# A hybrid decoder step on one core: loads of three stages moved a stage ahead, and the first projection tile copied out of PSUM before it is scaled

## The chip, the cores and the metric

The kernel runs on one core of one Trainium2 chip, as one program in one launch. The metric is the device time of that program in microseconds. Before the change it is 3295.6 us, the median of three runs (3295.22, 3295.60 and 3301.45).

## The reference, cut to what matters

One inference step of a decoder trunk of two layers, for 1024 prompt tokens and 8 sample tokens (one each, with a past of 8192 positions). Layer 0 runs two mixers side by side on one input projection: S5, a diagonal state-space model with 32 groups of 64 states, and multi-head latent attention (MLA) with 16 heads. Layer 1 is windowed attention. Each layer ends in a gated MLP with a short convolution. All is float32. The change lies in layer 0:

```python
h = rmsnorm(x, norm_mix[layer])
z = h @ e_w_in[li]                      # 512 S5 columns, 384 query, 256 key/value latent, 32 rotary
u, xq, xkv, kr = z[..., :o1], z[..., o1:o2], z[..., o2:o3], z[..., o3:]
y_s5, hr, hi = s5_mixer(u, h0_re, h0_im, lam_re, lam_im, log_dt, b_re, b_im, c_re, c_im, d_skip, w_glu, b_glu)
q_nope, q_rope, ckv, k_rope = mla_project(xq, xkv, kr, pos, q_norm, w_uq, kv_norm)
o = mla_prompt_attn(q_nope, q_rope, ckv, k_rope, w_uk, w_uv)
mix = jnp.concatenate([y_s5, o], axis=-1) @ e_w_out[li]
# at the end of s5_mixer:
y = gelu(y); y = y * sigmoid(y @ w_glu + b_glu)
# mla_project normalises both latents:
q = rmsnorm(xq, q_norm) @ w_uq;  ckv = rmsnorm(xkv, kv_norm)
```

## The kernel before, in words

Tokens lie along the free dimension (NT = 1032 columns: 1024 prompt and 8 sample), features along the 128 partitions. The kernel is written by hand, engine by engine: each stage is one block, and in it each engine has its own list of instructions with waits on semaphores. A block ends when all five engines have come to its end, so a stage opens on all engines at nearly one time. SP issues nearly all the DMAs, in the order in which they are written.

The stages that matter, in their order:

1. **First projection** (lines 273 to 462). Ten tiles of 128 columns of the weight matrix. SP loads a tile's weights into one of two slots of `slab_raw` (`Slabs.load`, L111). GpSimd splits them into a high and a low part (`Slabs.split`, L121 and L123) once the products that used the slot are done. TensorE makes three products for each of 8 slices of k and 3 thirds of the tokens (`Slabs.products`, L137 to L139), into one of two PSUM slots, which it takes when `slabs.free` says that the slot was emptied. VectorE empties a tile and scales it by the norm's factor `rstd` in one instruction (`evacuate`, L399). Tile q is computed as column tile (q + 4) % 10, so the latents come first. The norm's sums of squares are made on TensorE (`norm_sums`, L232) between the products of tile 1; their roots on ScalarE (`norm_roots`, L237, three thirds), their reciprocals on VectorE (L244). VectorE's list is then: `evacuate(0)`, six doublings of S5's table of cosines and sines (`double`, L409 to L414), `evacuate(1)`, a doubling, `evacuate(2)`, and so on. `scale` (L422) norms the latents and counts `lat_done`. SP stores the normed latents and the rotated key at the end (L305, L307).
2. **S5** (lines 473 to 793). SP first loads the four parameters `s5_b`, `s5_c`, `s5_d` and `s5_h0` (L503). TensorE waits for all of them (L515), transposes `s5_b` (L518), multiplies the samples by it (64 small matmuls, L523); VectorE waits for that (L656), then builds the tables of powers up to `ca` (L725), for which `slab_raw` serves as scratch. Four rounds of states follow (TensorE L564 to L588, VectorE L743 to L775), then the samples (L602 to L607), and ScalarE's gelu (L627, L631). SP ends with the stores of the states.
3. **Gate** (lines 796 to 832). SP loads the weights and the bias (L804, L805). TensorE waits for both and makes 4 column tiles of the product (L815), ScalarE their sigmoid (L824), VectorE the product with S5's output (L832).
4. **Heads** (lines 848 to 1116). A loop of four rounds with four heads each. SP loads the mask and the rotary table (L895, L896) and, at each round, the round's weights `wq` and `wkv` (L899, L900), once the nine projections of the round before are done (`proj` starts at 1, L918). TensorE waits for the weights (L935), projects queries (L924), keys (L931) and values (L952), and then runs the attention.

Then come the samples' attention over the paged cache, the output projection, the MLP and layer 1, which the diff doesn't touch. The change also moves names of buffers: all SBUF behind `z` is placed by hand in slots of 1032 floats (`at`, `placer`).

Of the kernel before, what the change touches and what calls it, by code (L numbers as in the profile page):

```python
# [28 lines left out]
P = 128  # L29
# [3 lines left out]
NS = 8  # L33
# [109 lines left out]
def build(nc, A, O):  # L143
    with ExitStack() as outer:
# [127 lines left out]
        C3 = float(2 * np.pi - C1 - C2)  # L272
        with ExitStack() as ctx:
# [13 lines left out]
                sem(n) for n in ("s5_tab_done", "kr_in", "kr_done", "lat_sq", "lat_added", "lat_sum", "lat_root", "lat_done"))  # L287
            swap_lanes = [q ^ 16 for q in range(32)]
            thirds = [slice(t * TT, (t + 1) * TT) for t in range(3)]
            evacuated = lambda eng, q: eng.wait_ge(slabs.free[q % 2], n0 + q // 2 + 2)  # L290
            with nc.Block() as block:
                @block.sync
                def _(sp):
# [10 lines left out]
                    sp.wait_ge(lat_done, 2)  # L304
                    store(sp, O["ckv"].rearrange("c p t -> p c t"), z[:, 7:9, :])  # L305
# [32 lines left out]
                def _(act):  # L338
# [27 lines left out]
                def _(dve):  # L366
# [65 lines left out]
                    evacuate(0)  # L432
# [35 lines left out]
        mix5 = zsb("mix5", [P, 4, NT])  # L468

# [3 lines left out]
        with ExitStack() as ctx:  # L473
            _, ps = scope(ctx)
            sb, late, few = placer(4), placer(27), placer(24)
            bw = sb("s5_b", [P, 4, 2, P])
            bpow = sb("s5_bpow", [P, LC, 2, NTILE5, 32])
            wst = sb("s5_wst", [P, LC - 1, 2, 4, P])
            ca = sb("s5_ca", [P, LC, 2, NTILE5, 32])
            hh = late("s5_hh", [P, 2, 2, 4, NC5 + 4])  # L480
# [4 lines left out]
            bus, dskip, h0 = few("s5_bus", [P, 2, NTILE5, NS]), few("s5_d", [P, 4]), few("s5_h0", [P, 2, NTILE5, NS])  # L485
            cw, czw = late("s5_c", [P, NTILE5, 2, 32]), late("s5_cz", [P, 2, NTILE5, 32])
            x8, hs, nhi = sb("s5_x8", [P, 4, NTILE5, NS]), few("s5_hs", [P, 2, NTILE5, NS]), few("s5_nhi", [P, NTILE5, NS])
# [308 lines left out]
        with ExitStack() as ctx:  # L796
            sb, ps = scope(ctx)
            wg, bg, gate = sb("glu_w", [P, 4, 4, P]), sb("glu_b", [P, 4]), sb("glu_gate", [P, 4, NT])
            out = ps("glu_out", [P, 2, 3, 512])
            w_in, mm_done, gate_done = sem("glu_w_in"), sem("glu_mm_done"), sem("glu_gate_done")  # L800
            with nc.Block() as block:
                @block.sync
                def _(sp):
                    sp.dma_start(wg[:, :, :, :], A["s5_wglu"].rearrange("m p k c -> p m k c")).then_inc(w_in, 16)  # L804
                    sp.dma_start(bg[:, :], A["s5_bglu"]).then_inc(w_in, 16)  # L805

                @block.tensor
                def _(pe):
                    pe.wait_ge(w_in, 32)
# [10 lines left out]
                def _(act):  # L820
                    act.wait_ge(w_in, 32)
# [24 lines left out]

        rot_in = sem("rot_in")
        HG, QK = 4, NOPE + ROPE
        with ExitStack() as ctx:
            sb, ps = scope(ctx)  # L850
            wq, wkv = sb("mla_wq", [P, 3, 3 * P]), sb("mla_wkv", [P, 2, 4 * P])
            qg, kg, vg = sb("mla_q", [QK, HG, NT]), sb("mla_k", [QK, HG, T]), sb("mla_v", [P, QB, HG * DV])
            qraw, ra, rb = sb("mla_qraw", [P, NT]), z[:, 0, :], z[:, 1, :]
            mask = sb("mla_mask", [P, 2, P])
# [7 lines left out]
            w_in, mask_in, proj = sem("mla_w_in"), sem("mla_mask_in"), sem("mla_proj")  # L862
# [29 lines left out]
            with nc.Block() as block:  # L892
                @block.sync
                def _(sp):
                    sp.dma_start(mask[:, :, :], A["masks"]).then_inc(mask_in, 16)  # L895
                    sp.dma_start(rot[:, :, :], A["rot_mla"]).then_inc(rot_in, 16)  # L896
                    with sp.Fori(0, 4) as gi:
                        sp.wait_ge(proj, gi * NPROJ + 1)
                        sp.dma_start(wq[:, :, :], A["w_uq"][bass.ds(gi, 1)].rearrange("a p k c -> p (a k) c")).then_inc(w_in, 16)  # L899
                        sp.dma_start(wkv[:, :, :], A["w_ukv"][bass.ds(gi, 1)].rearrange("a p k c -> p (a k) c")).then_inc(w_in, 16)  # L900
# [16 lines left out]
                def _(pe):  # L917
                    pe.sem_inc(proj, 1)  # L918
                    MM = nc.tensor.matmul
                    with pe.Fori(0, 4) as gi:  # L920
# [14 lines left out]
                        pe.wait_ge(w_in, gi * 32 + 32)  # L935
# [1350 lines left out]
```

## Time and profile before

| what | value |
|---|---|
| the three runs | 3295.22, 3295.60, 3301.45 us |
| profiled execution, its own time | 3301.38 us |
| its span, first to last instruction | 3299.6 us |
| mean granted TensorE clock | 0.963 |
| TensorE busy | 3030.4 us, 92% |
| VectorE busy | 1754.2 us, 53% |
| ScalarE busy | 714.6 us, 22% |
| GpSimd busy | 920.1 us, 28% |
| DMA, mean | 62 GB/s |

In the page's second part the span is cut into 40 slices of 82 us, each with a digit for tenths of busy time. TensorE's row reads `6956899998888879999999999997979999999996`: the first four slices, which hold stages 1 to 3 above, and the start of stage 4 are the emptiest. In a timeline a row has the start in us from the span's start, the time in us from the start of the first to the end of the last of the instructions merged in it, engine, line, operation, output <- input, the count, and in brackets how long the engine stood idle before it and what released it. SPq rows are DMA issues. L1013's and L1054's rows belong to stage 4, L1170's and L1191's to the stage behind it. Engine names are those of the page: PE is TensorE, PEld its weight loads, DVE VectorE, ACT ScalarE, POOL GpSimd, SP SyncE.

### The profile page before, as it was taken

To read this page: it belongs to the slowest core of one execution; us is meant where nothing else is said; L and a number is where in the kernel's file an instruction comes from. 1 tells how busy PE (TensorE), PEld (TensorE's weight loads), DVE (VectorE), ACT (ScalarE), POOL (GpSimd) and SP (SyncE) were. 2 spreads that over 40 slices of the span, in tenths; PEclk is the share of its full clock that TensorE was granted. 3 is DMA by queue.
4 is the path that set the end of the run, shared out by engine and by line. 5 is a ranking of instruction groups with operands and counts; after the bars stand their busy time and mean duration, and the time that the engine had idled before them with its cause. 6 is when DMAs were issued, how large, how long until landed. Compare 5 with 4: busy or idle time off the path is not lost. (4 is left out here: it accounts for less than half of the span.)

```text
span 3299.6 us, 58631 instructions
## 1 busy us (share of the span) xinstructions
PE 3030.4 (92%) x22071; PEld 2717.3 (82%) x22071; DVE 1754.2 (53%) x2759; ACT 714.6 (22%) x1510; POOL 920.1 (28%) x560
## 2 busy tenths in 40 slices
PE   6956899998888879999999999997979999999996
PEld 6844566667666669999999999995579999999996
DVE  8695556654555542751533435756836524435254
ACT  3111345543333320210000001204613100001001
POOL 3200001101111124443344343530024443443442
PEclk9977999998999979999999999998989999999998
DMA  2100100003766631111111111212111111111112
GB/s 98 52 1 15 42 14 0 14 26 93 202 195 194 193 113 48 57 41 54 45 40 51 42 53 39 66 39 73 51 48 57 43 46 51 42 50 39 54 38 74
DMA packets 129107, 205.64 MB, mean 62 GB/s; under 512 B 14833, under 2 KB 95729, under 8 KB 128274
## 3 DMA queue, kind: packets, MB, share of 16 engines
q1 hardware_dynamic: 127858, 200.07, 20.2%
q10 hardware_dynamic: 1152, 4.23, 0.3%
q8 instruction: 67, 1.10, 0.1%
q14 instruction: 30, 0.25, 0.0%
HBM read 189.87 MB, written 6.25 MB: 59 GB/s over the span
## 5 line engine op out<-in xcount | busy, mean ns | idle before, releaser
L137 PE MATMUL ps_trunk_out<-sb_h_hi,sb_slab_hi 128*128 128x344 f32 x2400 | 769.4, 321 | 0.0
L138 PE MATMUL ps_trunk_out<-sb_h_hi,sb_slab_lo 128*128 128x344 f32 x2400 | 766.0, 319 | 0.0
L139 PE MATMUL ps_trunk_out<-sb_h_lo,sb_slab_hi 128*128 128x344 f32 x2400 | 765.9, 319 | 0.0
L121 POOL TENSOR_TENSOR sb_slab_hi<-sb_slab_raw,sb_ones 128x1024 fp32r<-128x1024 f32 (+3 forms) x214 | 345.0, 1612 | 1371.7 <-PE ps_trunk_out L139 1052.1
L123 POOL TENSOR_TENSOR sb_slab_lo<-sb_slab_raw,sb_slab_hi 128x1024 fp32r<-128x1024 f32 (+3 forms) x214 | 489.2, 2286 | 16.8
L137 PEld LDWEIGHTS ps_trunk_out<-sb_h_hi,sb_slab_hi 128*128 128x128 f32 x2400 | 451.2, 188 | 0.6
L138 PEld LDWEIGHTS ps_trunk_out<-sb_h_hi,sb_slab_lo 128*128 128x128 f32 x2400 | 451.0, 188 | 0.6
L139 PEld LDWEIGHTS ps_trunk_out<-sb_h_lo,sb_slab_hi 128*128 128x128 f32 x2400 | 451.0, 188 | 0.0
L137 PE MATMUL ps_trunk_out<-sb_ffn_a_hi,sb_slab_hi 128*128 128x344 f32 x1056 | 337.5, 320 | 4.9 <-DVEq L1572 4.9
L139 PE MATMUL ps_trunk_out<-sb_ffn_a_lo,sb_slab_hi 128*128 128x344 f32 x1056 | 338.5, 321 | 0.0
L138 PE MATMUL ps_trunk_out<-sb_ffn_a_hi,sb_slab_lo 128*128 128x344 f32 x1056 | 336.8, 319 | 0.0
L1525 ACT ACTIVATE sb_ffn_a<-sb_ffn_c 128x1032 f32<-128x1032 f32 x44 | 47.0, 1067 | 997.3 <-DVEq L1562 997.3
L1581 DVE TENSOR_TENSOR sb_z<-sb_z,ps_trunk_out 128x1032 f32 x48 | 59.0, 1229 | 300.6 <-PE ps_trunk_out L139 300.6
L912 POOL TENSOR_TENSOR sb_mla_diag<-sb_ident,sb_mla_rinv 128x256 f32<-128x256 f32 x64 | 39.2, 612 | 594.8 <-DVE sb_mla_rinv L1093 594.8
L137 PEld LDWEIGHTS ps_trunk_out<-sb_ffn_a_hi,sb_slab_hi 128*128 128x128 f32 x1056 | 198.8, 188 | 6.0 <-DVEq L1572 6.0
L139 PEld LDWEIGHTS ps_trunk_out<-sb_ffn_a_lo,sb_slab_hi 128*128 128x128 f32 x1056 | 198.8, 188 | 0.0
L138 PEld LDWEIGHTS ps_trunk_out<-sb_ffn_a_hi,sb_slab_lo 128*128 128x128 f32 x1056 | 198.7, 188 | 0.0
L1549 DVE TENSOR_TENSOR sb_ffn_g<-ps_trunk_out,sb_rstd 128x1032 f32<-128x1032 f32 x44 | 54.2, 1233 | 232.3 <-PE ps_trunk_out L139 232.3
L964 PE MATMUL ps_mla_bank<-sb_mla_k,sb_mla_q 96*128 96x512 f32 (+3 forms) x384 | 150.2, 503 | 1.8 <-ACT sb_mla_v L1024 1.8
L1300 POOL TENSOR_TENSOR sb_dec_kr<-sb_dec_ck,sb_ones 128x256 f32<-128x256 f32 x64 | 46.6, 728 | 357.1 <-DMA sb_dec_ck<-cache 223.9
L1217 PE MATMUL ps_dec_bank<-sb_ident,sb_dec_ck 128*128 128x128 f32 x1024 | 134.3, 275 | 0.0
L1564 DVE TENSOR_TENSOR sb_ffn_u<-sb_rstd,ps_trunk_out 128x1032 f32<-128x1032 f32 x44 | 54.1, 1229 | 135.3 <-PE ps_trunk_out L139 135.0
(399 smaller groups left out, 5167.0 us busy)
## 6 DMA issues: line engine op xcount, KB each, us to landing
sb_dec_ck<-cache SPq DMA_DIRECT2D x512, 144.0 KB, 2.4
sb_slab_raw<-f_w_gu SPq DMA_DIRECT2D x88, 512.0 KB, 3.5
sb_slab_raw<-f_w_down SPq DMA_DIRECT2D x32, 384.0 KB, 3.0
sb_slab_raw<-f_w_down SPq DMA_DIRECT2D x32, 320.0 KB, 2.8
sb_slab_raw<-e_w_out SPq DMA_DIRECT2D x24, 256.0 KB, 2.6
sb_slab_raw<-o_w_in SPq DMA_DIRECT2D x12, 512.0 KB, 3.6
sb_slab_raw<-e_w_in SPq DMA_DIRECT2D x10, 512.0 KB, 3.3
sb_x_first<-x SPq DMA_DIRECT2D x8, 516.0 KB, 8.8
```

The costliest lines, as they stand in the source:

```text
L121: nc.gpsimd.tensor_tensor(hi, raw, one, ALU.mult).then_inc(self.hi_done[s], 1)
L123: nc.gpsimd.tensor_tensor(self.lo[:, s, 0:kc, :], raw, hi.bitcast(F32), ALU.subtract).then_inc(self.split_done[s], 1)
L137: nc.tensor.matmul(out[:, t, 0:TT], a, x_hi(k)[:, cols], start=k == 0, stop=False)
L138: nc.tensor.matmul(out[:, t, 0:TT], b, x_hi(k)[:, cols], start=False, stop=False)
L139: last = nc.tensor.matmul(out[:, t, 0:TT], a, x_lo(k)[:, cols], start=False, stop=k == kc - 1)
L964: m = MM(score(u)[:, c0:c1], qg[:, h, qb * P:(qb + 1) * P], kg[:, h, c0:c1], start=True, stop=True)
L1217: m = nc.tensor.transpose(bank[:, b % 4, k * P:(k + 1) * P], src, ident[:, :])
L1300: nc.gpsimd.tensor_tensor(kr[:, c % 2], ck[:, c % SLOTS, :, KVL:CW], one, ALU.mult).then_inc(kr_done, 1)
L1525: nc.scalar.activation(a[:, :], c[:, :], ACT.Gelu_apprx_tanh).then_inc(ffn_act_done, 1)
L1549: ch.link(V.tensor_tensor(v3(g[:, 2:]), slabs.out[:, 0, :, 0:TT], v3(rstd), ALU.mult))
L1564: ch.link(V.tensor_tensor(v3(u[:, :]), v3(rstd), slabs.out[:, 1, :, 0:TT], ALU.mult))
L1581: V.tensor_tensor(xm, xm, slabs.out[:, s, :, 0:TT], ALU.add).then_inc(slabs.free[s], 1)
```

## The change

- S5's four parameters are loaded in the first projection's stage, behind the wait for both latents, ahead of the store of the latents, into memory that the latents' norms have left. S5's waits for them stay.
- The gate's bias is loaded at S5's start and its weights, into `slab_raw`, once VectorE has finished `ca`. The gate's stage no longer loads them.
- The rotary table, the first round's `wq` and `wkv` and the mask are loaded in the gate's stage. In the heads' stage SP's loop runs three times and loads the next round's weights. `proj` starts at 0, and all waits for it are lower by 1.
- ScalarE copies tile 0 from PSUM to `z` as soon as it is complete, ahead of the norm's roots, and frees the slot. VectorE scales it in place where it emptied it before; ScalarE's square of tile 0 waits for that.
- Buffers are placed accordingly (`mixa`, `mla_qs`, `wq`, `wkv`, the mask and the rotary table are declared earlier).

```diff
@@ first projection
+        late = placer(27)
+        bw, cw = late("s5_b", [P, 4, 2, P]), late("s5_c", [P, NTILE5, 2, 32])
+        dskip, h0 = late("s5_d", [P, 4]), late("s5_h0", [P, 2, NTILE5, NS])
...
                     sp.wait_ge(lat_done, 2)
+                    for dst, src in ((bw[:, :, :, :], "s5_b"), (cw[:, :, :, :], "s5_c"), (dskip[:, :], "s5_d"),
+                                     (h0[:, :, :, :], "s5_h0")):
+                        sp.dma_start(dst, A[src]).then_inc(par_in, 16)
                     store(sp, O["ckv"].rearrange("c p t -> p c t"), z[:, 7:9, :])
...
                         norm_act(act, 0, k, x[:, k, :], gain(k), acc[:, :], sq[:, :])
+                    act.wait_ge(slabs.mm_done[0], n0 + 2)
+                    nc.scalar.copy(v3(z[:, tile(0), :]), slabs.out[:, 0, :, 0:TT]).then_inc(slabs.free[0], 1)
                     norm_roots(act, 0, tot, D)
                     for q, dst in enumerate((q_acc, q_r, kv_r, kv_acc, sq)):
-                        evacuated(act, q)
+                        if q == 0:
+                            act.wait_ge(first_done, 1)
+                        else:
+                            evacuated(act, q)
...
-                    evacuate(0)
+                    dve.wait_ge(slabs.free[0], n0 + 2)
+                    V.tensor_tensor(z[:, tile(0), :], z[:, tile(0), :], rstd[:, :], ALU.mult).then_inc(first_done, 1)
@@ between the first projection and S5
+        def fetch_heads(sp, gi):
+
+            for dst, src in ((wq, "w_uq"), (wkv, "w_ukv")):
+                sp.dma_start(dst[:, :, :], A[src][bass.ds(gi, 1)].rearrange("a p k c -> p (a k) c")).then_inc(mla_in, 16)
+        bg, glu_in = at("glu_b", 26, [P, 4], skip=3968), sem("glu_w_in")
+        wg = slabs.raw.rearrange("p s k c -> p (s k c)").rearrange("p (m k c) -> p m k c", m=4, k=4)
@@ S5
-                    for dst, src in ((bw[:, :, :, :], "s5_b"), (cw[:, :, :, :], "s5_c"),
-                                     (dskip[:, :], "s5_d"), (h0[:, :, :, :], "s5_h0")):
-                        sp.dma_start(dst, A[src]).then_inc(par_in, 16)
+                    sp.dma_start(bg[:, :], A["s5_bglu"]).then_inc(glu_in, 16)
+                    sp.wait_ge(ca_done, 1)
+                    sp.dma_start(wg, A["s5_wglu"].rearrange("m p k c -> p m k c")).then_inc(glu_in, 16)
                     sp.wait_ge(hs_done, 1)
@@ gate
-                    sp.dma_start(wg[:, :, :, :], A["s5_wglu"].rearrange("m p k c -> p m k c")).then_inc(w_in, 16)
-                    sp.dma_start(bg[:, :], A["s5_bglu"]).then_inc(w_in, 16)
+                    sp.dma_start(rot[:, :, :], A["rot_mla"]).then_inc(rot_in, 16)
+                    fetch_heads(sp, 0)
+                    sp.dma_start(mask[:, :, :], A["masks"]).then_inc(mask_in, 16)
...
-                    pe.wait_ge(w_in, 32)
+                    pe.wait_ge(glu_in, 32)
@@ heads
-                    sp.dma_start(mask[:, :, :], A["masks"]).then_inc(mask_in, 16)
-                    sp.dma_start(rot[:, :, :], A["rot_mla"]).then_inc(rot_in, 16)
-                    with sp.Fori(0, 4) as gi:
-                        sp.wait_ge(proj, gi * NPROJ + 1)
-                        sp.dma_start(wq[:, :, :], A["w_uq"][bass.ds(gi, 1)].rearrange("a p k c -> p (a k) c")).then_inc(w_in, 16)
-                        sp.dma_start(wkv[:, :, :], A["w_ukv"][bass.ds(gi, 1)].rearrange("a p k c -> p (a k) c")).then_inc(w_in, 16)
+                    with sp.Fori(0, 3) as gi:
+                        sp.wait_ge(proj, gi * NPROJ + NPROJ)
+                        fetch_heads(sp, gi + 1)
...
-                    pe.sem_inc(proj, 1)
...
-                        pe.wait_ge(w_in, gi * 32 + 32)
+                        pe.wait_ge(mla_in, gi * 32 + 32)
```

## Rows read from the trace of the kernel before

**Rows 1.** Waits of TensorE: waiter <- releaser: total us, times, longest us.

```profile
PE ps_mla_bank L924 <- DMA sb_mla_wkv<-w_ukv: 13.5, 1, 13.5
PE ps_s_bank L518 <- DMA sb_s_h<-s_h: 6.8, 1, 6.8
PE ps_w_in_out L137 <- DVE sb_z L399: 6.7, 1, 6.7
PE ps_glu_out L815 <- DMA sb_glu_b<-s_bglu: 6.0, 1, 6.0
```

**Rows 2.** Timeline, all engines, end of the first projection and start of S5.

```profile
151.96 0.31 PE L139 MATMUL ps_w_in_out<-sb_h_lo,sb_slab_hi 128*128 128x344 f32 x1
...
153.81 0.34 SPq L505 DMA_DIRECT2D sb_s_b<-s_b  x1
...
159.08 1.97 PE L518 MATMUL ps_s_bank<-sb_ident,sb_s_b 128*128 128x128 f32 x8 [6.80 <-DMA sb_s_h<-s_h]
...
164.64 0.49 DVE L658 COPY sb_s_bus<-ps_s_bank 128x128 f32<-128x128 f32 x2 [4.71 <-PE ps_s_bank L523]
```

**Rows 3.** Timeline, all engines, end of S5 and start of the gate.

```profile
290.87 0.20 ACT L631 ACTIVATE sb_mix<-ps_s_bank 128x32 f32<-128x32 f32 x1 [0.22 <-PE ps_s_bank L607]
291.32 0.39 SPq L804 DMA_DIRECT2D sb_glu_w<-s_wglu  x1
...
296.81 30.38 PE L815 MATMUL ps_glu_out<-sb_mix,sb_glu_w 128*128 128x344 f32 x96 [6.01 <-DMA sb_glu_b<-s_bglu]
```

**Rows 4.** Timeline, all engines, start of the heads' stage.

```profile
332.14 0.34 SPq L895 DMA_DIRECT2D sb_mla_mask<-masks  x1
332.28 2.28 DVE L1054 COPY sb_mla_k<-sb_z 32x4096 f32<-32x4096 f32 x1 [0.39 <-PEq L801]
...
340.70 18.47 PE L924 MATMUL ps_mla_bank<-sb_z,sb_mla_wq 128*128 128x344 f32 x54 [13.51 <-DMA sb_mla_wkv<-w_ukv]
```

**Rows 5.** Timeline, all engines, start of the stage behind the heads.

```profile
773.71 0.29 SPq L1170 DMA_DIRECT2D sb_dec_page_row<-pages  x1
...
774.06 2.60 PE L1191 MATMUL ps_dec_bank<-sb_mla_qs,sb_z 64*128 64x8 f32 x20 [1.40 <-PEq L892]
```

**Rows 6.** Timeline, SP, end of the first projection.

```profile
136.23 0.40 SPq L181 DMA_DIRECT2D out_ckv<-sb_z  x1
```

**Rows 7.** Timeline, all engines, tiles 0 and 1 of the first projection.

```profile
35.84 1.89 POOL L121 TENSOR_TENSOR sb_slab_hi<-sb_slab_raw,sb_ones 128x1024 fp32r<-128x1024 f32 x1 [14.72 <-PE ps_w_in_out L139]
...
37.78 1.13 ACT L237 ACTIVATE sb_rstd<-ps_w_in_extra,sb_eps 128x344 f32<-128x344 f32 x2 [2.56 <-PE ps_w_in_extra L232]
...
43.78 2.30 DVE L244 RECIPROCAL sb_rstd<-sb_rstd 128x344 f32<-128x344 f32 x1 [0.95 <-ACT sb_rstd L237]
46.12 1.23 DVE L399 TENSOR_TENSOR sb_z<-ps_w_in_out,sb_rstd 128x1032 f32<-128x1032 f32 x1
...
48.98 1.89 POOL L121 TENSOR_TENSOR sb_slab_hi<-sb_slab_raw,sb_ones 128x1024 fp32r<-128x1024 f32 x1 [8.77 <-PE ps_w_in_out L139]
```

**Rows 8.** Timeline, ScalarE, a table load at the gate and a copy at the heads.

```profile
306.45 1.28 ACT L824 ACT_TABLE_LOAD   x1 [15.39 <-PE ps_glu_out L815]
307.75 1.12 ACT L824 ACTIVATE sb_glu_gate<-ps_glu_out,sb_glu_b 128x1032 f32<-128x1032 f32 x1
...
348.80 1.02 ACT L1013 COPY sb_mla_qraw<-ps_mla_bank 128x1032 f32<-128x1032 f32 x1 [15.07 <-PE ps_mla_bank L924]
```

**Rows 9.** Stretches (A:B us): length, PE, PEld, DVE, ACT, POOL busy, PEclk, DMA, GB/s.

```profile
154.00:155.00 1.00, 0.00 (x0) 0.00 (x0) 0.43 (x5) 0.00 (x0) 0.00 (x0) 0.91 0.27 53
...
159.00:165.00 6.00, 5.50 (x72) 5.07 (x72) 1.23 (x6) 3.92 (x4) 0.00 (x0) 0.50 0.00 1
...
291.00:292.00 1.00, 0.00 (x0) 0.00 (x0) 0.00 (x0) 0.06 (x1) 0.00 (x0) 0.67 0.00 0
...
301.00:302.00 1.00, 1.00 (x4) 0.66 (x3) 0.00 (x0) 0.00 (x0) 0.00 (x0) 0.71 0.00 0
...
345.00:346.00 1.00, 1.00 (x4) 0.55 (x3) 0.00 (x0) 0.00 (x0) 0.00 (x0) 0.52 0.00 0
```

More of the change, by code:

```diff
@@ L468, in build @@
         mix5 = zsb("mix5", [P, 4, NT])
+        mixa = zsb("mixa", [P, 8, NT])
+        qs = zsb("mla_qs", [NOPE + ROPE, H, NS])
+        sel = zsb("dec_sel", [P, H])
+        wukT = z[0:NOPE, 0:4, :].rearrange("p a t -> p (a t)")[:, 0:H * KVL].rearrange("p (h c) -> p h c", h=H)
+        wuv = slabs.raw.rearrange("p s k m -> p s (k m)")
+        dec_w_in, pages_in = sem("dec_w_in"), sem("dec_pages_in")
+        rotary = ExitStack()
+        outer.enter_context(rotary)
+        rot = rotary.enter_context(nc.sbuf_tensor("sb_rot_mla", [P, 2, NT], F32))
+        wq, wkv = (rotary.enter_context(nc.sbuf_tensor("sb_mla_" + n, s, F32)) for n, s in
+                   (("wq", [P, 3, 3 * P]), ("wkv", [P, 2, 4 * P])))
+        mask = rotary.enter_context(nc.sbuf_tensor("sb_mla_mask", [P, 2, P], F32))
+        mla_in, mask_in, rot_in = sem("mla_w_in"), sem("mask_in"), sem("rot_in")
+        def fetch_heads(sp, gi):
[3 more added lines that the diff above has]
+        wg = slabs.raw.rearrange("p s k c -> p (s k c)").rearrange("p (m k c) -> p m k c", m=4, k=4)
         with ExitStack() as ctx:
             _, ps = scope(ctx)
-            sb, late, few = placer(4), placer(27), placer(24)
-            bw = sb("s5_b", [P, 4, 2, P])
+            sb, few = placer(4), placer(24)
             bpow = sb("s5_bpow", [P, LC, 2, NTILE5, 32])
@@ L484, in build @@
             last, sp_out = few("s5_last", [P, 2, NTILE5]), few("s5_pout", [P, 2, NTILE5])
-            bus, dskip, h0 = few("s5_bus", [P, 2, NTILE5, NS]), few("s5_d", [P, 4]), few("s5_h0", [P, 2, NTILE5, NS])
-            cw, czw = late("s5_c", [P, NTILE5, 2, 32]), late("s5_cz", [P, 2, NTILE5, 32])
-            x8, hs, nhi = sb("s5_x8", [P, 4, NTILE5, NS]), few("s5_hs", [P, 2, NTILE5, NS]), few("s5_nhi", [P, NTILE5, NS])
+            bus, x8 = few("s5_bus", [P, 2, NTILE5, NS]), few("s5_x8", [P, 4, NTILE5, NS])
+            hs, nhi = few("s5_hs", [P, 2, NTILE5, NS]), few("s5_nhi", [P, NTILE5, NS])
             u4 = mix5[:, :, 0:T].rearrange("p m (j c) -> p m j c", j=LC)
@@ L796, in build @@
         with ExitStack() as ctx:
-            sb, ps = scope(ctx)
-            wg, bg, gate = sb("glu_w", [P, 4, 4, P]), sb("glu_b", [P, 4]), sb("glu_gate", [P, 4, NT])
+            _, ps = scope(ctx)
+            gate = at("glu_gate", 4, [P, 4, NT])
             out = ps("glu_out", [P, 2, 3, 512])
-            w_in, mm_done, gate_done = sem("glu_w_in"), sem("glu_mm_done"), sem("glu_gate_done")
+            mm_done, gate_done = sem("glu_mm_done"), sem("glu_gate_done")
             with nc.Block() as block:
@@ L1011, in _ @@
                     with act.Fori(0, 4) as gi:
+                        act.wait_ge(proj, gi * NPROJ + 1)
+                        nc.scalar.copy(split3(qraw[:, :]), bank[:, 0:3, 0:TT]).then_inc(act_ev, 1)
                         act.wait_ge(proj, gi * NPROJ + 2)
-                        nc.scalar.copy(split3(qraw[:, :]), bank[:, 0:3, 0:TT]).then_inc(act_ev, 1)
-                        act.wait_ge(proj, gi * NPROJ + 3)
                         for hh in range(2):
```

28 lines of the change are left out of this document (9 added, 19 removed).

## The prediction

> **What bounds the kernel now.** I read the page's first two parts first: TensorE is busy for 92% of the span, and the dips of its row lie in the first tenth. There a microsecond on the chain of any engine moves everything behind it, since nothing later waits for a clock or for another core. Next I read who TensorE waited for, and how long [rows 1]. Four single waits touch this change: 6.8 us for S5's parameters, 6.0 us for the gate's weights, 13.5 us for the first heads' projections (all three on a DMA), and 6.7 us for VectorE emptying a tile of the first projection. A wait's length isn't yet its worth: part of it passes while other engines close the stage before. So I read the timeline at each of the three stage starts, for the moment at which the stage opens (its first instruction on any queue) and the one at which TensorE begins. S5 opens at 153.81 with the first of four loads, and the first transpose begins at 159.08 [rows 2]. The gate's stage opens at 291.32, just after ScalarE's last piece of S5, and its matmuls begin at 296.81 [rows 3]. The heads' stage opens at 332.14 and begins at 340.70 [rows 4].
>
> How soon can a stage begin that waits for no load? One row shows it: the stage behind the heads opens at 773.71 on SP's queue, and TensorE begins at 774.06, 0.35 us later [rows 5]. I take 0.35 us for each of the three starts.
>
> **S5's parameters.** The four loads move out of S5's start to behind the wait for the latents in the stage before. Without them TensorE can begin at 153.81 + 0.35 = 154.16 in place of 159.08: 4.9 us. Behind its 8 transposes and 64 small matmuls stands VectorE, which reads their result at 164.64 and is then the engine that sets S5's pace [rows 2]; so the whole gain passes on. What is late next is that same work of TensorE, 164.64 - 159.08 = 5.6 us at the low clock. In their new place the loads are issued just ahead of the store of the latents, which is now issued at 136.23 [rows 6]. They took 159.08 - 153.81 = 5.3 us, so they land by about 142, some 12 us ahead of need; TensorE's last tiles cover them. Without that cover they would cost at most the 5.3 us again. SP is held up by four issues, under 2 us. Behind them stand only two stores, and these are waited for at S5's end.
>
> **The gate's weights.** They move into S5, behind the end of the tables that used the same memory. TensorE can begin at 291.32 + 0.35 = 291.67 in place of 296.81: 5.1 us. What is late next is ScalarE's last gelu, over at 291.07 [rows 3]. The loads have the rest of S5 as cover, its four rounds of states (5.5 us if it were gone). SP's new wait stands ahead of the two stores of S5's states, which become ready only at S5's end.
>
> **The first heads' projections, rotary table and mask.** They move into the gate's stage and were needed 8.6 us after their first issue [rows 4]; the gate's 30.4 us of matmuls cover them. TensorE can begin at 332.14 + 0.35 = 332.49 in place of 340.70: 8.2 us. What is late next is VectorE's last product of the gate and the way into the loop. VectorE's own copy there begins at 332.28 and is done 2.28 us later, ahead of its next need. The reload for heads 4 to 15 waits for the same nine projections as before: its count loses the initial 1, and the waits lose it too. I cost that at nothing.
>
> **First tile out of PSUM unscaled.** ScalarE copies tile 0 as soon as its products are done, and VectorE scales it later in SBUF. The 6.7 us wait of rows 1 looks like the target, but it is tile 3's, which waits for VectorE to empty tile 1. Tile 0 was emptied from 46.12 to 47.35 and tile 2, which takes over its PSUM, could not start before tile 1 was done at 48.98, which is when the splitting of tile 3's weights is released [rows 7]. So the earlier release buys nothing. VectorE's own instruction stays in its place, 1.23 us on the same elements. What it may cost: tile 0's products end at 35.84, the copy takes 1.02 us (the same shape out of PSUM, rows 8), and the table load for the root, 1.28 us [rows 8], now done ahead of the 2.56 us in which ScalarE waits for TensorE's sums, comes behind the copy. The first roots would begin at 35.84 + 1.02 + 1.28 = 38.14 instead of 37.78, 0.36 us late. VectorE's first two reciprocals move with them, but VectorE then still idles for part of the 0.95 us in which it waits for the third root, until 43.78. That root follows TensorE's last sums, which don't move. So I take 0, with 0 and 0.7 us as ends.
>
> The Trainium skill (ScalarE: Activation LUTs, What ACT_TABLE_LOAD costs) prices a switch of tables at about 2.66 us, as a load of 1.28 us and a drain of 1.38 us. By that the roots would be 1.74 us late and, less the 0.95 us of slack, VectorE 0.8 us late; the sum would be that much smaller. The trace doesn't bear it out: at the gate a load began at 306.45, took 1.28 us, and its activation followed at 307.75 [rows 8].
>
> **TensorE's clock.** At all three starts the loads' wait had let the granted clock fall to its lower level (0.5, 1.2 GHz), and the first matmuls ran at half speed. From the mixed microseconds [rows 9]: it fell at 154.82 and 291.34, and came back at 301.58 and 345.96. So the gate lost half of 301.58 - 296.81, 2.4 us, and the heads half of 5.26, 2.6 us. In S5 all 72 matmuls and transposes ran at 0.50. What comes back?
> - S5: if the clock still falls at 154.82, 0.66 us run at full speed, which saves 0.66. Ends: 0, and half of 5.6, 2.8.
> - Gate: it fell at the very opening of the stage, at most 0.7 us behind S5's last, tiny matmuls, whose end released ScalarE at 290.87 [rows 3]; so a gap that is short doesn't by itself keep it up. Ends 0 and 2.4; I take 1.0, below the middle for that row.
> - Heads: TensorE still stands still from the gate's last matmul (296.81 + 30.38 = 327.19) to 332.49, over 5 us. I take 0, with 2.6 gained and 0.9 lost as ends (a low clock for 1.8 us longer than in any of these rows).
>
> **Sum.** 4.9 + 5.1 + 8.2 = 18.2 us of starts, 0.7 + 1.0 + 0 of clock, 0 for the first tile: 19.9 us. The profiled execution took 3301.4 us (span 3299.6, 1.8 around it), so it would take 3281.5. It is 5.8 us above the median of the three runs, 3295.6 (3295.2 to 3301.5), and the change should take as much from either: 3275.7.
>
> **Rivals.**
> 1. *The clock holds through the short gaps.* After the change TensorE stands still for under 2 us at S5's start and about 1 us at the gate's. If the clock stays up there, S5 saves 2.1 more and the gate 1.4 more: 23.4 us, 3272.2. For it: after the first projection the clock outlived the last matmul, over at 152.27, by 2.55 us [rows 2, 9]. Against it: the fall at 291.34. The Trainium skill (TensorE: Matmul & The Clock Gate, Why this matters for your kernels) says to leave no long idle gaps between bursts, so by that rule these short ones would cost nothing; rows 9 agree at the first start and not at the second. Chance 0.15.
> 2. *Another wait takes the place of one load.* The entry itself (code, the loop's registers, a table load on ScalarE) may have been hidden by the DMA. If it hides the smallest or the largest of the three gains, 11.7 to 15.0 us are left: 3281 to 3284. For it: no row shows these three entries uncovered. Against it: at the heads' VectorE is at work 0.14 us after SP's first issue [rows 4], and rows 5 show TensorE at work after 0.35. Chance 0.12.
> 3. *Little or nothing.* The moved loads aren't what ended the waits, or the loads in their new place hold up the tail of the first projection, so that over two thirds is given back: 3289 to 3299. Each wait's releaser in rows 1 is a DMA, and no later stage waits for an absolute time. Chance 0.07.
> 4. *Slower.* The place is the gate and the projections after it: TensorE comes to the gate straight from tiny matmuls and might get no full clock there. The gate's matmuls, 28.0 us without the 2.4 lost, would take 56, 25.6 more than now; the query projections (18.47 us, rows 4, with 2.6 lost in them) 13.2 more. It decides from the point at which the low clock lasts about 40 us longer than now, since each microsecond of it costs half of one against the 19.9. Held through both it gives 3295.6 - 18.2 + 38.8 = 3316. Against it: in both stages the clock came back within 5.3 us of the first matmul [rows 9]. Chance 0.03.
>
> **How the numbers follow.** The forecast has 0.63, and the rivals 0.37 together. Starts without any entry (5.3 + 5.5 + 8.6 = 19.4) and the best ends of the clock give 19.4 + 2.8 + 2.4 + 2.6 = 27.2 us, from the lowest run: 3268. The worst ends (18.2 - 0.9 - 0.7 = 16.6 us), from the highest run, give 3285; that holds rival 1 and most of rival 2. A measurement of this kernel tells about 0.2%, 6.6 us, from no change: 3289 to 3302 counts as the same. Forecast and rivals 1 and 2 are all faster by more than that, 0.90; rival 3 is the same, 0.07; rival 4 is slower, 0.03.
>
> **What would show it.** In the changed profile the three waits on a DMA are gone from TensorE's list, and S5's first transpose, the gate's and the heads' first matmul stand within 0.5 us of the stage's first instruction. S5's first transpose lies near 154.2, the gate's matmuls begin near 286, the heads' near 321. Tile 3's wait of 6.7 us is still there, within 1 us. The ends of the three stages run ahead of those before by 5.6, 11.7 and 20 us, and the gap then stays. I'm wrong if one of the starts waits for something else for over 1 us, if the first tile shortens or lengthens tile 3's wait, or if a later stage gives time back.

## The result, and the profile after

The changed kernel takes **3275.9 us**, the median of four runs (3271.06 to 3279.56); the kernel before takes 3295.8 (3295.22 to 3301.45, four runs). The ratio is 0.9937, with a 95% interval of 0.9925 to 0.9948. The forecast was 3275.7.

The two profiled executions lie further apart than the medians: 3271.06 us against 3301.38 (spans 3269.3 and 3299.6), 30.3 us. The one of after was the fastest of its runs, the one of before among the slowest. So a term is read below between two points inside the span, and never from the whole.

Four of TensorE's waits in the first 375 us of the changed kernel (waiter <- releaser: total us, times, longest us):

```profile
PE ps_w_in_out L137 <- DVE sb_z L411: 6.7, 1, 6.7
PE ps_mla_bank L941 <- ACTq L1026: 5.4, 1, 5.4
PE ps_s_bank L554 <- PEq L295: 1.6, 1, 1.6
PE ps_glu_out L852 <- PEq L536: 0.6, 1, 0.6
```

The three waits on a DMA [rows 1] are gone. What is left at the three starts is the passage from one stage to the next (PEq and ACTq are the sequencers of TensorE and ScalarE): L295 and L536 are the blocks of the first projection and of S5, which end there, and L1026 is ScalarE's first step in the heads' stage. Tile 3's wait is unchanged at 6.7 us.

The timeline of all engines of the changed kernel: the loads' new places, and the starts of S5, the gate and the heads:

```profile
134.82 0.33 SPq L311 DMA_DIRECT2D sb_s_b<-s_b  x1
...
136.61 0.43 SPq L181 DMA_DIRECT2D out_ckv<-sb_z  x1
...
152.40 0.34 SPq L539 DMA_DIRECT2D sb_glu_b<-s_bglu  x1
152.45 1.06 PE L554 MATMUL ps_s_bank<-sb_ident,sb_s_b 128*128 128x128 f32 x8 [1.59 <-PEq L295]
153.45 2.08 PE L559 MATMUL ps_s_bank<-sb_z,sb_s_b 32*128 32x8 f32 x64
155.58 0.49 DVE L694 COPY sb_s_bus<-ps_s_bank 128x128 f32<-128x128 f32 x2 [1.49 <-PE ps_s_bank L559]
...
281.19 0.20 ACT L667 ACTIVATE sb_mix<-ps_s_bank 128x32 f32<-128x32 f32 x1 [0.23 <-PE ps_s_bank L643]
...
281.65 0.35 SPq L840 DMA_DIRECT2D sb_rot_mla<-rot_mla  x1
...
311.30 4.67 DVE L869 TENSOR_TENSOR sb_mix<-sb_mix,sb_glu_gate 128x1032 f32<-128x1032 f32 x4 [33.40 <-PE ps_glu_out L852]
...
316.36 2.28 DVE L1071 COPY sb_mla_k<-sb_z 32x4096 f32<-32x4096 f32 x1 [0.40 <-PEq L837]
```

The loads of S5's parameters are issued 17.6 us ahead of S5's opening. S5's transposes begin 0.05 us behind the stage's first instruction, where they began 5.27 us behind it [rows 2], and VectorE reads the samples' product 3.18 us behind it instead of 10.83. The same view of TensorE alone, from the gate on:

```profile
281.70 29.57 PE L852 MATMUL ps_glu_out<-sb_mix,sb_slab_raw 128*128 128x344 f32 x96 [0.57 <-PEq L536]
316.62 18.74 PE L941 MATMUL ps_mla_bank<-sb_z,sb_mla_wq 128*128 128x344 f32 x54 [5.35 <-ACTq L1026]
335.19 5.31 PE L948 MATMUL ps_mla_bank<-sb_z,sb_mla_wkv 128*128 128x512 f32 x12
```

The gate begins 0.05 us behind its opening [rows 3: 5.49], and the heads' queries 0.26 us behind VectorE's copy [rows 4: 8.42]. The pause of 5.35 us ahead of the heads holds VectorE's four products (4.67 us from 311.30). The keys' first matmul (335.19) stood at 359.01 before, 18.31 us behind the queries' start [rows 4]:

```profile
359.01 3.17 PE L931 MATMUL ps_mla_bank<-sb_z,sb_mla_wkv 128*128 128x512 f32 x7
```

Single microseconds of the changed kernel (A:B us: length, PE, PEld, DVE, ACT, POOL busy, granted clock, DMA, GB/s):

```profile
155.00:156.00 1.00, 0.52 (x16) 0.43 (x12) 0.42 (x3) 1.00 (x1) 0.00 (x0) 0.58 0.00 0
...
278.00:279.00 1.00, 1.00 (x18) 0.43 (x10) 0.00 (x0) 0.04 (x1) 0.00 (x0) 0.98 0.36 83
...
281.00:282.00 1.00, 0.43 (x17) 0.36 (x6) 0.00 (x0) 0.20 (x1) 0.00 (x0) 0.73 0.00 0
...
284.00:285.00 1.00, 1.00 (x3) 0.62 (x2) 0.00 (x0) 0.00 (x0) 0.00 (x0) 0.56 1.00 421
...
322.00:323.00 1.00, 1.00 (x4) 0.65 (x3) 0.00 (x0) 0.00 (x0) 0.00 (x0) 0.79 0.00 0
```

In S5 the clock fell only at 155.16 (0.58 = 0.16 + 0.84 / 2), when 2.7 of TensorE's 3.1 us of work there (152.45 to 155.53) were done. At the gate it was low from 281.46 to 284.88, and at the heads until 322.42, 5.8 us behind the first matmul.

Two later rows answer to [rows 5]: the stage behind the heads opens at 749.90 and TensorE begins at 750.24, 23.8 us earlier than before, exactly the 23.8 us by which the keys run ahead (359.01 - 335.19). The heads' stage gives nothing back.

The first tile, in the rows of ScalarE, VectorE and TensorE of the changed kernel:

```profile
35.83 1.02 ACT L361 COPY sb_z<-ps_w_in_out 128x1032 f32<-128x1032 f32 x1 [1.88 <-PE ps_w_in_out L139]
36.87 1.28 ACT L237 ACT_TABLE_LOAD   x1
38.16 0.98 ACT L237 ACTIVATE sb_rstd<-ps_w_in_extra,sb_eps 128x344 f32<-128x344 f32 x2
...
43.78 2.30 DVE L244 RECIPROCAL sb_rstd<-sb_rstd 128x344 f32<-128x344 f32 x1 [0.57 <-ACT sb_rstd L237]
46.11 1.23 DVE L445 TENSOR_TENSOR sb_z<-sb_z,sb_rstd 128x1032 f32<-128x1032 f32 x1
...
66.79 0.62 PE L137 MATMUL ps_w_in_out<-sb_h_hi,sb_slab_hi 128*128 128x344 f32 x1 [6.68 <-DVE sb_z L411]
```

The roots begin at 38.16 (forecast 38.14), VectorE's slack shrinks from 0.95 to 0.57 us, and the last reciprocal stands at 43.78 as before [rows 7].

### The profile page after: what moved, and what is told of

It reads as the page before. It is cut to its first block and busy times, and to the rows that moved or that the text cites. A ratio compares the mean times of both kernels' runs of the same rounds, so it can differ in the third digit from the quotient of the medians.

```text
span 3269.3 us, 58624 instructions
## 1 busy us (share of the span) xinstructions
PE 3021.2 (92%) x22071; PEld 2709.9 (83%) x22071; DVE 1754.2 (54%) x2759; ACT 715.4 (22%) x1511; POOL 919.8 (28%) x560
```

## The experiments

All times by the same points of each trace, in us from the span's start: VectorE's read of the samples' product in S5, the first matmul of the gate, of the heads' queries, of the keys and of the stage behind the heads, and the span.

| kernel | S5 read | gate | queries | keys | behind heads | span |
|---|---|---|---|---|---|---|
| before | 164.64 | 296.81 | 340.70 | 359.01 | 774.06 | 3299.6 |
| after | 155.58 | 281.70 | 316.62 | 335.19 | 750.24 | 3269.3 |
| x1, after again | 156.31 | 282.88 | 317.92 | 335.02 | 750.11 | 3275.3 |
| x2, parameters late | 164.94 | 291.20 | 326.14 | 344.74 | 759.81 | 3281.5 |
| x3, gate late | 156.57 | 288.63 | 324.53 | 341.89 | 756.97 | 3271.7 |
| x4, heads late | 156.71 | 283.61 | 326.02 | 344.50 | 759.58 | 3281.0 |
| x5, tile alone | 164.25 | 296.11 | 339.05 | 357.29 | 772.34 | 3294.5 |
| x6, emptied early | 153.25 | 279.82 | 313.17 | 330.34 | 745.38 | 3269.2 |
| x7, gap filled | 156.62 | 283.36 | 318.40 | 334.11 | 749.15 | 3267.9 |
| x8, both | 153.32 | 279.93 | 313.27 | 328.99 | 744.04 | 3269.7 |
| x9, roots first | 148.06 | 273.94 | 307.29 | 323.01 | 738.04 | 3260.3 |
| x10, gate filled | 155.92 | 284.57 | 317.92 | 336.22 | 751.25 | 3273.9 |

From the stage behind the heads to the end, the code is the same in all twelve, apart from where buffers lie, and yet that stretch takes between 2514.7 us (x3) and 2525.7 (x8). That spread of 11 us is as large as a term; the keys' column is not touched by it. x1 to x4 ran on one chip and x5 to x10 on another, so each ratio is taken against the kernel before on the same chip.

**x1: the changed kernel once more.** No edit.

> The changed kernel itself, once more, to have it beside the runs that undo one part each. Theory (three stage starts): 19.9 us below the kernel before, as at first, within 3 us. Rival (part of the first difference was luck of the runs, the profiled pair differs by 30.3 us): anything from 12 to 30 us. In its profile the three waits on a DMA are absent.

Median 3273.8 us (3272.4 to 3277.6, five runs) against 3297.4; ratio 0.993 (0.9917 to 0.9943). The keys' column agrees with the first profile within 0.2 us, while the spans differ by 6.0: that difference comes from behind the heads. The agreement at the keys is partly chance: the queries begin 1.3 us later in x1 and take 1.5 us less. Timelines of x1, S5's start, and TensorE from the gate on:

```profile
153.23 0.33 SPq L539 DMA_DIRECT2D sb_glu_b<-s_bglu  x1
...
156.31 0.49 DVE L694 COPY sb_s_bus<-ps_s_bank 128x128 f32<-128x128 f32 x2 [1.39 <-PE ps_s_bank L559]
...
282.88 29.69 PE L852 MATMUL ps_glu_out<-sb_mix,sb_slab_raw 128*128 128x344 f32 x96 [1.93 <-PEq L536]
...
317.92 17.27 PE L941 MATMUL ps_mla_bank<-sb_z,sb_mla_wq 128*128 128x344 f32 x54 [5.35 <-ACTq L1026]
```

The following three are set against this run.

**x2: S5's parameters loaded at S5's start again.**

```diff
@@ first projection, SP
-                    for dst, src in ((bw[:, :, :, :], "s5_b"), (cw[:, :, :, :], "s5_c"), (dskip[:, :], "s5_d"),
-                                     (h0[:, :, :, :], "s5_h0")):
-                        sp.dma_start(dst, A[src]).then_inc(par_in, 16)
@@ S5, SP: the same three lines, ahead of
                     sp.dma_start(bg[:, :], A["s5_bglu"]).then_inc(glu_in, 16)
```

> The changed kernel with S5's four parameters loaded at S5's start again. Theory: S5 opens, and VectorE reads the small products some 10.8 us later instead of 3.2, as before the change; the run is 5.3 us (start alone) to 7.7 us (start and clock) slower than the changed kernel, near 3282. Rival (the loads ahead of the latents' store hold up the end of the first projection and gave part back): less than 4 us slower. Rival (S5's later rounds make up for a late start): less than 2 us slower.

3284.8 us (3282.0 to 3286.9), ratio 0.9963 (0.995 to 0.9976): 11.0 us above x1 by the medians, more than expected. The timeline of x2 at S5's start:

```profile
153.63 0.34 SPq L538 DMA_DIRECT2D sb_s_b<-s_b  x1
...
159.38 1.97 PE L554 MATMUL ps_s_bank<-sb_ident,sb_s_b 128*128 128x128 f32 x8 [7.29 <-DMA sb_s_h<-s_h]
161.28 3.60 PE L559 MATMUL ps_s_bank<-sb_z,sb_s_b 32*128 32x8 f32 x64
...
164.94 0.49 DVE L694 COPY sb_s_bus<-ps_s_bank 128x128 f32<-128x128 f32 x2 [4.71 <-PE ps_s_bank L559]
```

From the opening to VectorE's read it takes 11.31 us; in x1 it takes 3.08 (opening 153.23). So this part is worth **8.2 us**: 5.7 of entry (5.75 against 0.05) and 2.5 because TensorE's 72 small products run at the upper clock (5.56 us from the first of them to the read here, 3.03 there). The rest of the 9.7 us at the keys is the queries' clock, 18.60 us against 17.10, and an opening 0.4 later, less 0.4 between the read and the queries; none of it is this edit's.

**x3: the gate's weights loaded in the gate's stage again.**

```diff
@@ S5, SP
-                    sp.dma_start(bg[:, :], A["s5_bglu"]).then_inc(glu_in, 16)
-                    sp.wait_ge(ca_done, 1)
-                    sp.dma_start(wg, A["s5_wglu"].rearrange("m p k c -> p m k c")).then_inc(glu_in, 16)
@@ gate, SP, ahead of the rotary table
+                    sp.dma_start(wg, A["s5_wglu"].rearrange("m p k c -> p m k c")).then_inc(glu_in, 16)
+                    sp.dma_start(bg[:, :], A["s5_bglu"]).then_inc(glu_in, 16)
```

> The changed kernel with the gate's weights and bias loaded at the gate's start again. Theory: the gate's first matmul comes 5.4 us after the stage's opening and runs at the low clock for about 5 us, so 5.4 to 6.5 us slower than the changed kernel, near 3282. The heads' loads follow behind on the same queue and are still covered by the gate's 30 us of matmuls, so the heads start without a wait. Rival (the heads' loads were what mattered in that stage): no difference over 2 us.

3282.0 us (3273.5 to 3290.1, six runs), ratio 0.9958 (0.9946 to 0.9969); 8.2 above x1. Timelines of x3, the gate's opening and TensorE:

```profile
283.01 0.38 SPq L837 DMA_DIRECT2D sb_slab_raw<-s_wglu  x1
...
288.63 30.55 PE L851 MATMUL ps_glu_out<-sb_mix,sb_slab_raw 128*128 128x344 f32 x96 [7.40 <-DMA sb_glu_b<-s_bglu]
```

The stage opened at 283.01: 5.6 us of start in place of 0.05, and 0.9 us more of low clock (30.55 against 29.69 in x1). **6.4 us**, as expected. The heads' loads stayed hidden although they are issued behind these: the queries begin 0.25 us behind VectorE's copy as in x1.

**x4: the first heads' loads at the heads' start again.**

```diff
@@ gate, SP
-                    sp.dma_start(rot[:, :, :], A["rot_mla"]).then_inc(rot_in, 16)
-                    fetch_heads(sp, 0)
-                    sp.dma_start(mask[:, :, :], A["masks"]).then_inc(mask_in, 16)
@@ heads, SP: the same three lines, ahead of
                     with sp.Fori(0, 3) as gi:
```

> The changed kernel with rotary table, mask and the first round's weights loaded at the heads' start again. Theory: the heads' first matmul comes 8.4 us after VectorE's first copy instead of 0.3, and the low clock lasts as long as now, so 8 us slower than the changed kernel, near 3284. Rival (entry work of the loop or the table load ends as late as the loads): under 5 us slower. The three undone parts together should make 18.2 to 22 us; if they sum to under 16, a part of the gain has another source, the first tile being the one that is left.

3283.7 us (3280.4 to 3286.1), ratio 0.9959 (0.9946 to 0.9972); 9.8 above x1. Timelines of x4, heads' start:

```profile
318.40 2.29 DVE L1072 COPY sb_mla_k<-sb_z 32x4096 f32<-32x4096 f32 x1 [0.40 <-PEq L837]
...
326.02 18.64 PE L942 MATMUL ps_mla_bank<-sb_z,sb_mla_wq 128*128 128x344 f32 x54 [12.72 <-DMA sb_mla_wkv<-w_ukv]
```

7.62 us from VectorE's copy to the first matmul, 0.25 in x1: **7.4 us**, and 1.4 more of clock (18.64 against 17.27). The three parts by themselves are worth 8.2 + 6.4 + 7.4 = 22.0 us, the upper end of what was expected. The medians add up to more, 11.0 + 8.2 + 9.8 = 29.0 us against the 23.6 of x1: each of them holds its own clock at the queries and its own stretch behind the heads, and each ratio is known to about 4 us only. So the parts are read from the traces.

**x5: the first tile's part alone**, on the kernel before.

```diff
+                    act.wait_ge(slabs.mm_done[0], n0 + 2)
+                    nc.scalar.copy(v3(z[:, tile(0), :]), slabs.out[:, 0, :, 0:TT]).then_inc(slabs.free[0], 1)
                     norm_roots(act, 0, tot, D)
...
-                    evacuate(0)
+                    dve.wait_ge(slabs.free[0], n0 + 2)
+                    V.tensor_tensor(z[:, tile(0), :], z[:, tile(0), :], rstd[:, :], ALU.mult).then_inc(first_done, 1)
```

> The kernel before with the first tile's part of the change alone: ScalarE copies tile 0 out of PSUM, VectorE scales it in SBUF. Theory: within 2 us of the kernel before (the roots begin 0.4 us later, the third reciprocal stays where it is, tile 3 still waits 6.7 us for tile 1 to be emptied). Rival (freeing the slot early lets TensorE run on): 3 to 7 us faster, with a shorter wait at tile 3. Rival (late table load, by a price of 2.66 us for the switch): up to 0.8 us slower and the wait at tile 3 longer by as much.

3296.5 us (eleven runs) against 3296.5 (fifteen); ratio 1.0001 (0.9992 to 1.001). It is worth nothing, within about 3 us. TensorE's waits in x5 hold tile 3's as before:

```profile
PE ps_w_in_out L137 <- DVE sb_z L405: 6.7, 1, 6.7
```

**x6: tile 1 emptied early.** On the changed kernel, the rest of VectorE's order moved with it. This attacks the wait that the first tile's part left.

```diff
                     for j in range(6):
+                        if j == 2:
+                            evacuate(1)
                         double(j, 0, 1 << j)
-                    evacuate(1)
-                    double(6, 0, 64)
                     evacuate(2)
-                    double(7, 0, 64)
+                    double(6, 0, 64)
                     evacuate(3)
-                    double(7, 64, 128)
-                    dve.sem_inc(tab_done, 1)
                     added(0, q_acc, q_r, 2)
                     added(1, q_acc, kv_r, 3)
+                    double(7, 0, 64)
                     evacuate(4)
+                    double(7, 64, 128)
+                    dve.sem_inc(tab_done, 1)
                     added(2, kv_acc, sq, 5)
```

> The changed kernel with VectorE's list in another order: it empties tile 1 behind the second doubling instead of behind the sixth, tile 2 ahead of the seventh, tile 4 ahead of the last, and makes the two sums of the query latent's squares ahead of the eighth. The same instructions. Theory (tile 3's wait hangs on VectorE's order, not on tile 0): the wait of 6.7 us disappears and with it the low clock behind it (half speed for 3 to 6 us, so 1.5 to 3 us): 8 to 9.7 us faster than the changed kernel, near 3267. Rival (GpSimd's splitting, which holds VectorE up, or a later tile's emptying takes the wait over): under 4 us faster, with a new wait of TensorE on VectorE in the first projection.

3271.0 us (3267.5 to 3273.2) against 3296.5; ratio 0.9917 (0.9903 to 0.9931). At the keys it is 4.7 us ahead of x1, half of what was expected. Only 3.1 of them are there at S5's read; 1.7 come at the gate, where the clock stayed up in x6 (28.00 us for the 96 matmuls, 29.69 in x1). Tile 3's wait is gone from TensorE's waits, and this one is new:

```profile
PE ps_w_in_extra L330 <- ACT sb_q_r L374: 3.9, 1, 3.9
```

ScalarE's timeline of x6 shows why:

```profile
103.06 1.06 ACT L370 ACTIVATE sb_x_sq<-sb_z 128x1032 f32<-128x1032 f32 x1 [25.31 <-DVEq L461]
104.03 0.97 ACT L374 ACTIVATE sb_q_r<-ps_w_in_extra,sb_eps 128x344 f32<-128x344 f32 x2
```

The queries' roots (L374) stand on ScalarE behind the last square of the latents, which waits for VectorE's table (L461), because it is written into that table's scratch. TensorE, now ahead, stood in tile 6 for those roots.

**x7: the pause ahead of the heads filled** with 8 matmuls behind the gate's last, into PSUM that nobody reads.

```diff
                         last_mm.then_inc(mm_done, 1)
+                    for q in range(8):
+                        nc.tensor.matmul(idle[:, 0:TT], wg[:, 0, 0, :], z[:, 4, 0:TT], start=True, stop=True)
```

> The changed kernel with 8 more matmuls of 344 columns behind the gate's last one, into a bank that nothing reads, 0.57 us each at full speed: they fill 4.6 of the 5.4 us in which TensorE stands still ahead of the heads. Theory (what is left of the heads' loss is the clock alone): the granted clock stays at 1.00, the heads' 54 query matmuls take 15.7 us instead of 18.7, 2.9 us faster than the changed kernel. Rival (the clock falls whatever fills the gap, or the stage's entry is held up by the extra work): no difference, or up to 1 us slower.

3272.0 us (3265.8 to 3274.0) against 3296.5; ratio 0.9919 (0.9906 to 0.9933). TensorE's timeline of x7:

```profile
312.89 4.79 PE L857 MATMUL ps_glu_idle<-sb_z,sb_slab_raw 128*128 128x344 f32 x16
318.40 15.88 PE L944 MATMUL ps_mla_bank<-sb_z,sb_mla_wq 128*128 128x344 f32 x54 [0.72 <-ACTq L1029]
```

The query projections take 15.88 us in place of 18.74 (after) or 17.27 (x1): 2.9 or 1.4 us gained, by how long the clock had stayed low in each. They take 15.88 in x8 and x9 too, which fill the pause as well, and 17.3 us or more in every run that doesn't. In the whole, 0.9919 against x1's 0.993, the intervals overlap.

**x8: x6 and x7 together.**

> The changed kernel with VectorE's other order and the 8 extra matmuls together. Theory: the two add up, 8 to 9.7 and 2.9 us: 11 to 12.6 us faster than the changed kernel, near 3264. Rival (they don't both hold): as the better one alone.

3271.5 us (3260.8 to 3272.6) against 3296.5; ratio 0.9911 (0.9895 to 0.9927). At the keys 6.0 us ahead of x1: x6's 4.7 and 1.4 of clock add up there. In the whole it is level with x6 (0.9917), and the 11 to 12.6 us of the theory were not reached. The 3.9 us wait is there again.

**x9: the queries' roots ahead of the last square**, on x8 (`lat_roots` is the loop of the roots, made a function).

```diff
                         if q == 4:
+                            lat_roots(0, q_r, QL)
                             act.wait_ge(tab_done, 1)
...
-                    added(2, kv_acc, sq, 5)
                     evacuate(5)
+                    added(2, kv_acc, sq, 5)
```

> The kernel of x8, in which ScalarE takes the roots of the query latents ahead of the last square of the latents, and VectorE empties tile 5 ahead of the last sum. In x6 and x8 TensorE stood 3.9 us in tile 6 for those roots, which queued on ScalarE behind that square, and the square waited for VectorE's table. Theory: the 3.9 us wait goes, S5 opens near 146 us in place of 149.9, the queries' first matmul lies 4 us earlier than in x8 (309.3), and the whole is 3 to 5 us faster than x8. Rival: VectorE, nearly without a pause from tile 2 on, is the next bound; another wait takes the place, S5 opens near 149 and the whole is within 1 us of x8.

3263.9 us (3259.9 to 3268.9) against 3299.5; ratio 0.9898 (0.9882 to 0.9915). The wait is gone, S5 opens at 144.18 in place of 149.91, and the queries begin 6.0 us ahead of x8, where 4 were expected. The stop in x8 had cost clock as well, as two microseconds of x8 show (columns as above):

```profile
104.00:105.00 1.00, 0.22 (x1) 0.25 (x2) 0.77 (x1) 1.00 (x3) 0.00 (x0) 0.81 0.93 276
...
108.00:109.00 1.00, 1.00 (x7) 1.00 (x7) 1.00 (x2) 0.00 (x0) 0.00 (x0) 0.98 0.18 70
```

It was low from 104.62 to 108.04, 1.7 us lost, and 3.9 + 1.7 = 5.6 us is nearly the whole difference of 5.7 at S5's opening. TensorE's timeline of x9:

```profile
273.94 28.00 PE L857 MATMUL ps_glu_out<-sb_mix,sb_slab_raw 128*128 128x344 f32 x96 [0.57 <-PEq L540]
301.78 4.79 PE L861 MATMUL ps_glu_idle<-sb_z,sb_slab_raw 128*128 128x344 f32 x16
307.29 15.88 PE L948 MATMUL ps_mla_bank<-sb_z,sb_mla_wq 128*128 128x344 f32 x54 [0.72 <-ACTq L1033]
```

At the keys it is 12.0 us ahead of x1: 8.3 are there at S5's read, 0.7 come up to the gate's start, 1.7 from the gate's clock and 1.4 from the queries'. By the ratios it is 0.993 - 0.9898 = 0.32% of 3296, 10.5 us. It beats both kernels.

**x10: the pause ahead of the gate filled** with 4 matmuls behind S5's last, on the changed kernel.

```diff
                     mm.then_inc(ys_done, 1)
+                    for q in range(4):
+                        MM(bank[:, 3, 0:TT], wst[:, 0, 0, 0, :], u4[:, 0, :, :].rearrange("p a b -> p (a b)")[:, 0:TT], start=True, stop=True)
```

> The changed kernel, with 4 matmuls of 344 columns behind S5's last, into a part of PSUM that is read by nobody any more (nothing is left out). They fill the 0.57 us in which TensorE stood still ahead of the gate. Theory: the clock fell there because of that pause; with it filled, the gate's 96 matmuls take 28.0 us at full clock in place of 29.57, 1.6 us less. Rival: the fall doesn't hang on that pause, and the low stretch of 3.2 us comes all the same, at or behind the gate's start: 29.5 us for the gate's matmuls, and no difference in the whole. By the whole time alone neither can be told from noise (1.6 us is 0.05%).

3274.9 us (3272.0 to 3279.3) against 3299.5; ratio 0.993 (0.9913 to 0.9946), the same as x1. TensorE's timeline of x10:

```profile
281.69 2.58 PE L647 MATMUL ps_s_bank<-sb_mix,sb_s_wst 128*128 128x344 f32 x8
284.57 28.00 PE L854 MATMUL ps_glu_out<-sb_mix,sb_slab_raw 128*128 128x344 f32 x96 [0.30 <-PEq L536]
```

The pause shrank to 0.30 us, the clock stayed up and the gate took 28.00 us in place of 29.57, as the theory says. But in x6, x8 and x9 it took 28.00 with the 0.57 us left empty, so this run alone doesn't show that the filling did it. And the four matmuls ran as eight instructions, 2.58 us in all, and held the stage's end to 284.52; ScalarE was done at 282.03, and 0.26 us later the stage could have opened as in the changed kernel (281.39 to 281.65). So 1.6 us were bought for about 2.2.

## Why the prediction was right

**The cause** is shown: each load put back brings back its wait, at its place and with its releaser (x2, x3, x4), and the first tile alone moves nothing (x5). Rival 3 (little or nothing) and rival 4 (a low clock through gate and projections) are out: the gate and the queries worked at the lower level for 3.2 and 5.8 us, and no stretch of it comes near 40. Rival 2 was that the entry hides a wait of its own; none of the three starts has one, though in x1 the end of S5 held the gate up (last section). Rival 1 (the clock holds) came true for S5 almost wholly and for the gate not in this kernel.

**The sum**, term by term, between the profiles of before and after:

| term | forecast | measured |
|---|---|---|
| S5, opening to VectorE's read | 4.9 + 0.7 | 10.83 - 3.18 = 7.65 |
| gate, opening to first matmul | 5.1 | 5.49 - 0.05 = 5.44 |
| gate's matmuls, clock | 1.0 | 30.38 - 29.57 = 0.81 |
| heads, copy to first matmul | 8.2 | 8.42 - 0.26 = 8.16 |
| queries to keys, clock | 0 | 18.31 - 18.57 = -0.26 |
| first tile | 0 | 0 (x5: ratio 1.0001) |
| together | 19.9 | 21.8 |

- **Entry.** The 0.35 us from [rows 5] was too long for two of the three: it is 0.05 us at S5 and at the gate (0.3 us more gain each). At the heads the queries do begin about 0.4 us behind the opening (VectorE's copy followed SP's first issue by 0.14 us in [rows 4], and TensorE follows the copy by 0.26).
- **S5's clock** was the mis-sized term: 0.7 forecast, about 2.4 measured (5.56 us from the first transpose to VectorE's read [rows 2], 3.13 now), near the upper end of 2.8. The step that failed was that "the clock still falls at 154.82", as before, with TensorE at work from 154.16. It fell at 155.16, and TensorE had started at 152.45, so 2.7 us of its work ran at the upper level in place of 0.66. In x1, x3, x4, x7 and x10 the clock fell behind all of that work, between 155.92 and 157.62. The hour of the fall was not one to be read off a single execution: the clock outlived the last matmul of the first projection by 2.55 us before and by 4.9 us in x5, where the loads stand at S5's start as before.
- **Gate's clock**: 0.8 us for 1.0 here and 0.7 in x1; in x6, x8 and x9, where the gate opens earlier, the whole 2.4 (28.00 against 30.38). The 1.0 was chosen between 0 and 2.4 by one row, so that it came near is partly luck. The row that said a short gap doesn't keep the clock up [rows 3, 9] was right for the changed kernel.
- **Heads**: 0 us of clock for a pause of 5.35 us; right for this execution (x1 gained 1.2), and x7 shows that it is this gap that costs the clock.
- **First tile**: right by its own steps; the roots, the slack and tile 3's wait are where they were put.

The gate's and the heads' matmuls, forecast near 286 and 321, begin 4.3 us earlier, at 281.70 and 316.62. At the keys the profiled pair shows 23.8 us. The other 2.0 came from outside the terms: S5 opened 1.41 us earlier in this execution (152.40; with the same first projection 152.84 in x10 and 153.23 to 153.62 in x1, x4 and x7), and S5's middle was 0.61 shorter. The 6.5 us up to the 30.3 of the spans arise behind the heads, where nothing changed, within the 11 us of spread of the table. That 3275.9 met 3275.7 so closely is partly chance: x1's runs gave 23.6 us.

The Trainium skill (ScalarE: Activation LUTs, What ACT_TABLE_LOAD costs) would have put a drain behind the table load; the changed kernel's rows show the load 0.02 us behind the copy's end (35.83 + 1.02 = 36.85, 36.87) and the root 0.01 us behind the load's (36.87 + 1.28 = 38.15, 38.16). The measurement decides: no drain is seen here. Its advice against long idle gaps between bursts (TensorE: Matmul & The Clock Gate, Why this matters for your kernels) agrees with x7 at the heads; at the gate of the changed kernel the clock fell in a pause of only 0.57 us.

## What to carry to other kernels

Price a load that moves ahead of its stage from the stage's first instruction to the first that waited, not by the length of the wait: the waits here were 6.8, 6.0 and 13.5 us, the gains of the starts 5.2, 5.4 and 8.2. Add what the clock gives back: half of the time, at the lower level, of the work that then runs ahead of its fall; that fall differs from one execution to the next. Before you free a resource earlier, look whose release ends the wait: the first tile's PSUM was freed 10 us earlier for nothing, since the wait was for tile 1; putting that one forward (x6), and then the roots that came due behind it (x9), brought 8.3 of the 12.0 us at the keys, and the clock most of the rest. And measure small terms at a point of the trace right behind the change, where they are not drowned by the spread of the stages that follow.

## What the runs showed that was not expected

- **The clock at the gate doesn't follow the pause alone.** With the same pause of 0.57 us it fell in the changed kernel (281.46, 0.3 us behind the last small product; it had come up at 278.04) and in x2 (291.02), and did not in x6, x8 and x9. In x1 the pause was 1.93 us, the clock was 1.00 all through it, and fell at 283.20, 0.3 us after the gate's matmuls had begun; in x4 and x7 (pauses of 2.10 and 1.83 us) it fell behind the gate's start too. The rows of x1:

```profile
281.00:282.00 1.00, 0.00 (x0) 0.00 (x0) 0.00 (x0) 0.20 (x1) 0.00 (x0) 1.00 0.03 1
282.00:283.00 1.00, 0.12 (x1) 0.15 (x2) 0.00 (x0) 0.00 (x0) 0.00 (x0) 1.00 0.00 0
283.00:284.00 1.00, 1.00 (x3) 0.64 (x4) 0.00 (x0) 0.00 (x0) 0.00 (x0) 0.60 0.55 74
```

  With 0.30 us (x10) it held. What decides stays open.
- **S5 can end with a store.** In x1 ScalarE was done at 281.22, and the stage ended only when the store of the last states had landed. SP's waits of x1 show it:

```profile
SPq L536 <- DMA out_s_p<-sb_s_pout: 2.9, 1, 2.9
```

  That store took 3.2 us from issue (279.20) to landing in x1, and 3.1 to 3.4 in x3, x4 and x7, where the gate opened as late; in the other eight it took 1.6, with which it would have landed in x1 at 280.8, ahead of ScalarE's end. Why it took twice as long stays open. In x1 it ate up what a faster clock had given in S5's last round (4.98 us for 64 products, 6.38 in the first profile of the changed kernel): the gate opened 1.6 us behind ScalarE's end. The forecast had named ScalarE's last gelu alone as what is late next.
